# A two-layer hybrid block (pooling, state-space and attention heads): the events of one state-space chunk are placed over three attention units in place of two

## The reference, cut to what matters

```
Lmat = exp(segsum(a))                                     # decay between two tokens of a chunk
scores = einsum('bclhn,bcshn->bhcls', Cc, Bc) * Lmat      # masked scores
y_diag = einsum('bhcls,bcshp->bclhp', scores, x)
y_off = einsum('bclhn,bchpn,bhcl->bclhp', Cc, prev_states, exp(a_cs))
return (y_diag + y_off).reshape(Bsz, L, H, P), final
```

## Time and profile before

| what | value |
|---|---|
| median of 3 runs | 1577.48 us (1576.39 to 1578.38) |
| the profiled execution, its own time | 1579.55 us |
| its span | 1577.7 us |
| PE busy | 1525.2 us, 97% |
| DVE busy | 868.0 us, 55% |
| ACT busy | 595.0 us, 38% |
| POOL busy | 137.9 us, 9% |
| mixer stage with SSD chunks, first layer | about 203 to 269 us of the span |
| the same, second layer | about 1078 to 1121 us |

### The profile page before, as it was taken

How to read it: one execution, slowest core, us unless ns; L and a number is a source line. 1 busy time by engine, 2 the same in 40 slices (tenths; PEclk the granted TensorE clock), 3 DMA queues, 4 the chain that set the end, 5 groups by cost and what they waited for, 6 DMA issues and landing times.

```text
span 1577.7 us, 22083 instructions
## 1 busy us (share of the span) xinstructions
PE 1525.2 (97%) x8944; PEld 1376.2 (87%) x8944; DVE 868.0 (55%) x1174; ACT 595.0 (38%) x900; POOL 137.9 (9%) x150
## 2 busy tenths in 40 slices
PE   6999989999999999999999999998999999999998
PEld 4899867899999999999999998995778788888887
DVE  4678887546755555555553367448656333333333
ACT  6634377535422112221122345346646221222222
POOL 0230431020000000000000024023110000000000
PEclk9999999999999999999999999999999999999999
DMA  9556221023443333333332132312022333333322
GB/s 366 163 172 195 67 84 41 14 67 102 144 143 107 133 121 119 130 120 125 133 107 57 51 80 78 83 54 77 15 67 81 94 104 96 91 89 100 93 77 84
DMA packets 208105, 162.49 MB, mean 103 GB/s; under 512 B 9268, under 2 KB 191004, under 8 KB 207900
## 3 DMA queue, kind: packets, MB, share of 16 engines
q1 hardware_dynamic: 206588, 156.63, 32.1%
q10 hardware_dynamic: 1440, 4.78, 0.8%
HBM read 156.76 MB, written 2.15 MB: 101 GB/s over the span
## 4 chain that ended last, share of the span: by engine, by line
PE 83%; DVE 7%; ACT 5%; issue 3%; POOL 1%; DMA 0%; SPq 0%; DVEq 0%; ACTq 0%; POOLq 0%
PE banks L1874 70%; PE banks L1992 4%; PE banks L2143 2%; DVE w_lo L1295 1%; DVE mod_sum L1320 1%; PE banks L2021 1%; PE banks L2049 1%; PE banks L2120 1%; DVE neg_max L1675 1%; DVE nrm L1397 1%; PE banks L2176 1%; DVE h_lo L1391 1%; PE banks L1826 1%; ACT nrm L932 1%; ACT w_hi L879 0%
## 5 line engine op out<-in xcount | busy, mean ns | idle before, releaser
L1295 DVE TENSOR_TENSOR w_lo<-raw,w_hi 128x1056 fp32r<-128x1056 f32 x184 | 245.8, 1336 | 297.8 <-ACT w_hi L879 297.0
L1874 PE MATMUL banks<-h_hi,w_hi 128*128 128x384 f32 (+3 forms) x1296 | 387.0, 357 | 9.5 <-DVE h_lo L1391 4.3
L1874 PE MATMUL banks<-h_lo,w_hi 128*128 128x384 f32 (+3 forms) x1296 | 383.1, 354 | 0.0
L1874 PE MATMUL banks<-h_hi,w_lo 128*128 128x384 f32 (+3 forms) x1296 | 382.8, 354 | 0.0
L879 ACT ACTIVATE w_hi<-raw 128x1056 fp32r<-128x1056 f32 x184 | 198.4, 1078 | 244.6 <-PE banks L1874 227.3
L1874 PEld LDWEIGHTS banks<-h_hi,w_hi 128*128 128x128 f32 x1296 | 236.1, 189 | 39.0 <-DVE h_lo L1391 9.7
L1874 PEld LDWEIGHTS banks<-h_hi,w_lo 128*128 128x128 f32 x1296 | 238.3, 189 | 16.8
L1874 PEld LDWEIGHTS banks<-h_lo,w_hi 128*128 128x128 f32 x1296 | 237.8, 189 | 15.8
L1874 PE MATMUL banks<-g_hi,w_hi 128*128 128x384 f32 (+1 forms) x528 | 159.9, 357 | 0.0
L1874 PE MATMUL banks<-g_hi,w_lo 128*128 128x384 f32 (+1 forms) x528 | 159.4, 356 | 0.0
L1874 PE MATMUL banks<-g_lo,w_hi 128*128 128x384 f32 (+1 forms) x528 | 159.1, 355 | 0.0
(11 more groups left out here) (223 smaller groups left out, 1893.7 us busy)
## 6 DMA issues: line engine op xcount, KB each, us to landing
raw<-in_w_dram SPq DMA_DIRECT2D x120, 512.0 KB, 3.9
mod_ring<-in_w_mod_dram SPq DMA_DIRECT2D x96, 512.0 KB, 4.9
raw<-in_w_in_dram SPq DMA_DIRECT2D x32, 512.0 KB, 4.9
raw<-in_w_out_dram SPq DMA_DIRECT2D x16, 512.0 KB, 4.3
raw<-in_w_dram SPq DMA_DIRECT2D x16, 384.0 KB, 3.5
cb_rows<-cs_rows_dram SPq DMA_DIRECT2D x20, 256.0 KB, 3.4
x_in<-in_x_dram ACTq DMA_DIRECT2D x4, 512.0 KB, 8.2
out_dram<-x_out SPq DMA_DIRECT2D x8, 256.0 KB, 2.3
```

Of the source, the lines that this page charges most:

```text
L1295: dve.tensor_tensor(w_lo[n % 2][:, :], raw[n % 4][:, :], as_f32(w_hi[n % 2][:, :]), ALU.subtract).then_inc(lo_ready, 1)
L1874: ins = pe.matmul(to(p, a, b), ws[:, w], xs(k, a, b), start=(first and q == 0), stop=(last and q == 2))
```

## The change

The SSD work of a chunk is placed over three units. In odd unit u (`ssd`): D on DVE, the decay on ACT, `x_dt` and `e_cum` on POOL, as before. At the end of unit u+1 (`ssd_g`): G on PE; on DVE the two mask multiplications and behind them the two products. At the end of unit u+2, which is odd (`ssd_y`): y on PE and the two additions on DVE. The next chunk's `ssd` follows in the same unit, behind that. The separate event `ssd_w` is gone. The gated norm and the early splits start one unit later, since they start when no chunk is left.

```
@@ mixer_events
             for u in range(len(units) + 3):
-                if last_c is not None:
-                    ev.append(("ssd_w", last_c, u))
                 if u < len(units):
...
                 ev += in_unit.get(u, [])
                 gate_now = not todo and last_c is None
                 if last_c is not None:
-                    ev.append(("ssd_y", last_c))
-                    last_c = None
+                    ev.append(("ssd_y" if u % 2 else "ssd_g", last_c))
+                    last_c = None if u % 2 else last_c
@@ vector engine
                         ins.then_inc(d_ready, 1)
-                        dve.wait_ge(g_pe, l * INCS["g_pe"] + n_y + 1)
+                        n_y += 1
+                    elif e[0] == "ssd_g":
+                        dve.wait_ge(g_pe, l * INCS["g_pe"] + n_y)
                         for d, tri in ((0, tri_le), (1, tri_ge)):
                             dve.tensor_tensor(g_mask[:, d, :, :], banks[:, 6, 256:512].rearrange("p (g s) -> p g s", g=2),
                                               tri.unsqueeze(1).to_broadcast([P, 2, P]), ALU.mult).then_inc(gm_ready, 1)
-                        n_y += 1
-                    elif e[0] == "ssd_w":
-                        u = e[2]
-                        if scaled < u - 1:
-                            scale_probs(u - 1, units[u - 1][1])
-                            scaled = u - 1
                         dve.wait_ge(gm_ready, l * INCS["gm_ready"] + 2 * n_y)
                         for d in range(DIRS):
                             dve.wait_ge(e_ready, l * INCS["e_ready"] + 2 * n_y - 1 + d)
@@ tensor engine
-                    elif e[0] == "ssd":
+                    elif e[0] == "ssd_g":
                         cc = e[1]
                         if n_y == 0:
```

## The result

| | median | lowest to highest | runs |
|---|---|---|---|
| before | 1577.48 us | 1574.84 to 1579.29 | 11 |
| after | 1580.98 us | 1578.70 to 1582.32 | 11 |

The ratio after to before is 1.0024, with a 95% interval of 1.0017 to 1.0032. The prediction was 1573.0 us, faster; what came is 3.5 us slower, just above the range's upper end of 1580.5.

What follows compares the result with a forecast made beforehand. The chain decay, products, y was taken to set PE's pace in the mixer stage. Terms -1.0 - 2.1 - 2.5 + 0.7 + 0.4 = -4.5 us, from the median 1577.48, gave 1573.0 us, range 1567.5 to 1580.5.

Steps and rivals of the forecast that it cites:

- Net for the first layer 12.0 - 11.0 = 1.0 us faster: First layer's mixer: 12.0 us of PE's waiting could go, 11.0 us come back elsewhere, 1.0 us gained.
- 7.2 - 5.1 = 2.1 us faster: Second layer's mixer: 7.2 us in play, 5.1 us come back, 2.1 us gained if the clock stays up.
- 2.5 us faster: Ends of both attention stages: early splits one unit later leave 0.5 us of PE's waits, 2.5 us gained.
- the wait in unit 8: y of chunk 3, its masks and products behind `w_out_tile`: PE waits 2.8 us in the first layer, 1.8 in the second.
- the waits of units 5 to 12: First layer: five waits of 0.5 to 0.9 us for ACT's copy, two of 0.1 to 0.2 for DVE, 3.9 us.
- 1.0 us taken off for a slower y: First layer: y at 1.67 us, not the walk's 1.5, eats part of every wait, so 12.0 becomes 11.0 us.
- the clock of the second layer: Chunk 0, second layer: the slow clock may fall again and return 1.4 us; half was counted, 0.7 us.
- Chunk 0: First layer: PE waits 4.0 us for ACT's copy behind the first decay, and the slow clock costs 1.3 us.
- Where DVE and POOL meet: D on DVE beside POOL's `x_dt` in eight chunks: 0.2 us longer, bounds 0 and 0.61; 0.4 us in all.
- rival (D): Slower: decay starts over 1.0 us later after y than walked, `p_T` copies late; at 2.0 us 1581. Chance 0.13.
- What was in play: PE's removable waiting in the mixer, slow clock included: 12.0 us in the first layer, 7.2 in the second.
- the pauses within y: Within y, waits for the second product and POOL's `e_cum`: 4.8 us that can go.

Runs made afterwards that it cites:

- e1: The kernel after, with the weight tile's split in unit 8 placed behind G, masks and products in the list: 1575.29 us, ratio 0.9988 to before.
- e10: e1 without POOL's rotary work on heads 2 and 3, last queries, first layer (part of the computation left out): 1574.39 us, ratio 0.9981 to before.
- e9: e1 with DVE scaling the last unit's probabilities ahead of the second early `m_lo`, not behind it: 1572.09 us, ratio 0.9963 to before.
- e4: The kernel after, with ACT's decay moved behind its next copy of transposed probabilities: 1586.42 us, ratio 1.0063 to before.
- e13: e9 with ACT's decay moved behind its next copy of transposed probabilities: 1581.73 us, ratio 1.0033 to before.

## Why the prediction was wrong

**The failed step** is the one that the prediction put as "Net for the first layer 12.0 - 11.0 = 1.0 us faster": between the same landmarks the kernel after was 2.6 us slower. In the second layer "7.2 - 5.1 = 2.1 us faster" came out as 0.0, and "2.5 us faster" at the ends as 0.4. What it had wrong is what comes back: 11.0 us were put back in its sum, 14.1 were by the trace. Three terms make most of that up: the slow clock behind the wait in unit 8, put at nothing (1.4 us), the waits of units 5 to 12, put at 3.9 (4.8 us), and 1.0 us taken off for a slower y, for which the trace shows no ground. The sum of -4.5 was a small rest between two large numbers, and its three large parts erred the same way; only the clock of the second layer, put at +0.7, came out better.

1. **Unit 8, the clock behind it.** The wait was foreseen, in the first layer at too high a price: 2.8 and 1.8 us predicted, 2.08 and 1.87 measured. Missing was what it does to the clock: I had counted falls at chunk 0, where PE had been busy 0.43 of 2 us, and none here, where it was busy 1.85 of 4. It fell, in the first layer. Against e1 this adds 1.0 us behind y and 0.3 in y; against the same steps elsewhere S and the transposes behind y are 1.4 us longer. e1 shows the whole: without the wait 3.8 us are gone at this place. The place of the split also decides the sign: with the split behind the products the change is faster than before, with it ahead it is slower.
2. **The waits in units 5 to 12.** Foreseen 3.9 us. The waits of PE between 220 and 266 us, without the one behind the split, sum to 0.26 + 1.00 + 0.50 + 0.23 + 0.55 + 0.49 + 0.65 + 0.26 = 3.9 us. But the walk went by the starts of instructions, and by these the steps that they lengthen, without the 0.26 us within y, are 4.8 us longer. The division was off too: three of the waits (1.00, 0.55, 0.65) end 0.10 us behind ACT's copy of the probabilities, not five; two end behind other copies by ACT (0.23 and 0.49), and three are for DVE, of which 0.26 and 0.50 us are for the products themselves.
3. **Chunk 0.** Foreseen a wait of 4.0 us at about 212 us, measured 3.86 at 209.7. Foreseen 1.3 us of slow clock; the windows from 210 to 216 us stand at 0.73, 0.50 and 0.92, that is 0.5 + 1.0 + 0.2 = 1.7 us. In the second layer the clock stayed at 1.00 in the windows of chunk 0, the better of the two outcomes between which I took half. The four waits there, foreseen as 1.6, 1.2, 1.8 and 0.9 us, measured 1.22 and 1.42 (less the 0.79 that stood there before), 1.73, 1.87 and 0.70: 6.2 us where I wrote 5.1 after taking 0.5 off.
4. **Where DVE and POOL meet.** I costed D only, at 0.4 us. Grouped by line and shape (busy us, mean ns of one), the kernel before has

```profile
L1711 DVE TENSOR_TENSOR e_in<-e_in,g_mask 128x512 f32<-128x512 f32 x20 | 12.9, 687 | 5.9 <-ACT e_in L1174 5.9
L1694 DVE TENSOR_SCALAR e_in<-cb_rows,cs_tok 128x128 f32<-128x128 f32 x40 | 8.7, 279 | 0.0
```

and the kernel after

```profile
L1705 DVE TENSOR_TENSOR e_in<-e_in,g_mask 128x512 f32<-128x512 f32 x20 | 17.2, 897 | 0.3
L1692 DVE TENSOR_SCALAR e_in<-cb_rows,cs_tok 128x128 f32<-128x128 f32 x40 | 10.8, 332 | 0.0
```

   The products, moved from behind POOL's work to beside it, grew by 4.3 us and D by 2.1. D met `x_dt` in five of the eight chunks and took 1.22 to 1.60 us there, 0.86 in the others: 0.36 to 0.74 us more, where I had taken 0.2 with a bound of 0.61. The dearest of these meetings costs 1.5 us of the stage (e10). That is the step "the masks and products have left that place" of rival (D) turned round: I looked at what the products leave, and not at who works where they arrive.
5. **What was in play.** I took the 12.0 us by the starts of instructions, so what came back has to be taken in the same way: each step of PE from its start to the next one's, less what the same step takes undisturbed. By the timeline that is 4.0 us at chunk 0 and 1.7 for the clock behind it, 4.8 for item 2, 2.2 ahead of y in unit 8 and 1.4 for the clock behind it: 14.1 where I had 11.0. The 1.0 us that I took off, because y would take 1.67 us and not 1.5, had no ground: in three of the six chunks y took 1.46. Of the 12.0 went 7.0 ahead of y, 3.5 in y, 0.5 of slow clock and 0.6 behind the split: 11.6. So the reading of the pauses within y held; its six times add up to 13.6 us before and 10.1 after. And 14.1 - 11.6 = 2.5 of the 2.6 us by which the stage is slower.
6. **The ends.** I let the last scaling come ahead of the early split by time. It is issued by the event of its transposes, which the list holds behind the `m_lo` of the iteration before, whatever the time is. The wait stayed at 1.64 us (1.81 in two parts before) and 0.72 + 0.17 (1.24). e9, which puts the scaling ahead, wins 1.3 of the 2.5 us.
7. **Rival (D)** foresaw a time of 1581, and that is the time; its mechanism is there in part only, so the match is luck. From the moment when PE goes on behind y to ACT's next decay pass 0.1, 1.8, 2.2, 0.9 and 0.1 us in the first layer and 0.3, 1.2 and 0.1 in the second. In three of these eight chunks that is more than the 1.0 us by which, in my walk, it could be late for nothing, and behind each of the three PE waits for ACT's copy: 1.00, 0.55 and 1.73 us, 3.3 in all and not 8. Behind the other five there is one such wait, 0.65 us, where the transposes are those of a unit of context. One of the three (PE had gone on from y at 235.69):

```profile
237.87 0.62 ACT L1175 ACTIVATE e_cum<-cb_rows 64x512 f32<-64x512 f32 x1
...
241.38 0.60 ACT L1149 ACTIVATE p_T<-banks 128x512 f32<-128x512 f32 x1
...
242.07 0.84 PE L2015 MATMUL banks<-tab,probs 128*128 128x128 f32 x6 [0.55 <-issue]
```

   So the sign that the prediction named, a decay well after y, came true there. What makes the decay late is DVE: in all three ACT had sat idle for 3.0 to 3.7 us for DVE's maximum before the exponential that stands ahead of the decay. e4 and e13, in which the decay starts some 2.4 us or more after y in every chunk, cost some 6 and 11 us.

**What stays open.** The 1.2 us between the stages lie ahead of the second mixer, where the clock is low for longer. The windows of before and then of after:

```profile
1072.00:1074.00 2.00, 2.00 (x6) 1.14 (x6) 0.72 (x2) 1.59 (x2) 0.00 (x0) 0.91 0.31 66
```

```profile
1072.00:1074.00 2.00, 2.00 (x4) 0.97 (x3) 0.02 (x1) 1.29 (x2) 0.00 (x0) 0.50 0.47 94
```

Over the experiments this stretch took 777.0 to 779.6 us, with no code in it that differs. Whether the change moves it, or each execution finds the clock in another place, the single profiled executions can't tell; the same holds for what e9 won outside the stages.

## What to carry to other kernels

When all engines walk one list, a step that is moved to a later place is moved behind everything that stands between, on every engine: look there for an instruction that waits for another engine (here a weight split that held DVE for 4.5 us), and move the step's new place ahead of it. Ask too who works beside the moved step where it arrives, since the same DVE instruction took 0.69 us alone and up to 1.75 beside POOL. And where a forecast is a small difference of two large sums of waits, the sign is open: the order of two events, a wait of 2 us and the clock behind it turned this one.

## What the runs showed of the hardware

A product on DVE (128x512, both inputs in SBUF) took 683 to 693 ns in all 20 cases of the kernel before, and up to 1747 ns in the kernel after:

```profile
L1705 DVE TENSOR_TENSOR e_in<-e_in,g_mask x20: 679/692/1747, 209.9 to 1118.8; 128x512 f32<-128x512 f32 x20
```

POOL suffers too: `e_cum` rose from 771 to 871 ns in the mean. The Trainium skill, "SBUF — State Buffer", section "Who interferes with whom", says that a DVE instruction with two inputs in SBUF contends with a GpSimd instruction that reads SBUF. The trace agrees, and gives the size that the page doesn't: 2.5 times, at worst, for one product. The scaling, 0.62 us alone, ended 0.42 us behind the instruction of POOL beside it both times: 236.95 against 236.53 us, and in the kernel after 225.43 against 225.01, where it took 1.43 us. So some 0.2 us of it ran beside POOL, and the rest waited.

The granted clock fell to 1.2 GHz behind a stretch of 4 us in which PE was still busy 1.85 us, with no single wait over 2.1 us; in e1, at 3.59 of 4 us, it stayed at 2.4 GHz. In the second layer the wait of 1.87 us at the same place left the clock at 1.00 for the whole stretch from 1109 to 1122 us. So a wait of this length may or may not cost the clock.
